# Router logits taken from the unnormalised stream, their transposes placed between output units, first gathers placed between the first expert units

## The chip, the core and the metric

The kernel runs on one core of one Trainium2 chip. The metric is device time in microseconds (us), lower is better. TensorE is called PE in the rows, VectorE DVE, ScalarE ACT, GpSimd POOL, and SP is the engine that issues most of the weight loads. TensorE's granted clock has two levels, 1.2 and 2.4 GHz; the rows give it as a share, 0.50 or 1.00.

## What is computed

One layer of a hybrid encoder over 16 meta tokens and 256 tokens, width 2048. The part that matters here is its second half: an output projection, a layer norm, a router, and a mixture of experts.

```python
h = layer_norm(ALPHA * h + mix, ln1_g[l], ln1_b[l])          # mix ends in: merged @ w_out
...
xf = h.reshape(n_tok, d)
g_logits = (xf @ w_group).astype(jnp.float32)                 # 4 groups
g_sel = jnp.argmax(g_logits + b_group.astype(jnp.float32), axis=-1)
...
e_logits = (xf @ w_expert).astype(jnp.float32).reshape(n_tok, N_GROUPS, EXPERTS_PER_GROUP)[tok, g_sel]
_, e_local = lax.top_k(e_logits + e_bias, TOP_K)              # 2 of the group's 8 experts
...
return (jax.nn.silu(xb @ w1[e]) * (xb @ w3[e])) @ w2[e]       # per expert, 32 experts, inner width 512
```

After the experts come a weighted sum of each token's two results, a residual and a last layer norm.

## The kernel before

**Units.** Every weight matrix is read in units of 1 MB (128 partitions x 2048 fp32). SP loads a unit, ACT copies it to its high part (`wh`, function `hi`), DVE subtracts to get the low part (`wl`, function `lo`), and PE multiplies with both parts. Before the experts PE uses 24 matmuls of 512 columns for a unit, in the expert part 8 (4 in full fp32 for two unsplit units in 24, `XR`). The expert part has 384 units, 24 per pair of experts, in 16 pairs (`pair`), and a ring of 8 units (`RING2`) whose high parts have 4 places (`HELD`).

**Order.** Each engine has a fixed program, written out by hand; engines wait for each other by semaphores. Nothing is rescheduled. An engine that waits holds up everything that stands behind in its own program.

**Output stage.** 16 units of `w_out` in four groups of four (`for j in range(4)` in the PE block). Each group gives 512 columns of the stream for both 128-token tiles, into two PSUM banks. DVE's `copy_out(j)` copies them to `mrg` and takes bn_stats. Group 3's copy can start only when the last unit is done.

**Between the last output unit and the first expert unit.** DVE normalises `mrg` in place (three passes over two tiles: mean and deviation, gain, bias) and splits the result into `xh1` and `xl1`. PE transposes `mrg` (32 transposes, `tensor_experts`, L822), ACT copies them out (L502), and PE multiplies with the router weights `wr` (32 matmuls of 36 columns, L828). DVE then selects group and experts in small dependent steps (`first_max`), PE counts ranks (L833 to L835), and DVE writes the 0/1 matrix `pg` for the first pair of experts (`gather_matrix`, L679).

**Gathers.** `gather(g, q)` on PE picks the tokens of pair g with `pg` out of `xh1` and `xl1`: 8 matmuls of 128 columns for each q, and q runs from 0 to 7. ACT copies each result to `xg` (`gathered`, L517). Before, PE does all 8 for pair 0 ahead of the first unit, while DVE computes the combine weights (small steps, L689 to L716). The gathers of pair 1 stand between the units of pair 0 (`G_FIRST`), and so on. An up-unit u reads only the gathers 2u and 2u+1. `pg` is one buffer: the matrix of the next pair is written when the last gather of this pair is done.

**Expert loop.** In pair 0 the units are called 0 to 19 here (k = 0 to 3, then 8 to 23). At the end of unit 8 (k = 12) PE runs `mix` (16 small matmuls, L891), which stands once at the same place in each pair and so marks the pairs in time.

Of the kernel before, what the change touches and what calls it, by code (L numbers as in the profile page):

```python
# [13 lines left out]
P = 128  # L14
# [77 lines left out]
def moe_trunk(nc, ins, out):  # L92
# [15 lines left out]
    with ctx:  # L108
# [176 lines left out]
        h1t = place("h1t", [P, KD, SEQ], 147456)  # L285
# [14 lines left out]
        pg = place("pg", [P, TT, 2 * SLOTS], M0 + 6144, F32R)  # L300
# [14 lines left out]
        ex = place("ex", [P, TT, 2], K0 + 5120)  # L315
        slots2 = place("slots2", [P, 2 * SLOTS], K0 + 2560)
# [14 lines left out]
        s_h1 = sem("s_h1")  # L331
        s_xh1 = sem("s_xh1")
        s_xl1 = sem("s_xl1")
        s_h1t = sem("s_h1t")
        s_h1tc = sem("s_h1tc")
# [62 lines left out]
        G_FIRST = (1, 3, 8, 10, 16, 18, 20, 22)  # L398

        def sync_experts(sp):  # L400
            def load(turn, x, src):

                n = 24 * turn + x if isinstance(turn, int) else None
                if n is not None and n < RING2:
                    if n < 4:
                        sp.wait_ge(s_ob, 2 * RET_PAIRS + 1)
                    else:
# [51 lines left out]
        def stage_constants(pool):  # L459

            pool.wait_ge(s_m, 9)
            for dst, src in ((ln1g[:, :], ins["ln1_g"].broadcast_to([P, D_MODEL])),
# [7 lines left out]
                pool.dma_start(dst, src).then_inc(s_c2, 16)  # L470
            nc.gpsimd.iota(tokm[:, :], [[P, TT]], -OUTSIDE, 1,
                           allow_small_or_imprecise_dtypes=True).then_inc(s_tok, 1)

        def pool_experts(pool):
            def scatter(filled, par):

                pool.wait_ge(s_h1, 1)
# [19 lines left out]
        def scalar_experts(act):  # L497

            act.wait_ge(s_wused, N_UNITS)
            for b in range(KD):  # L500
                act.wait_ge(s_h1t, b + 1)
                nc.scalar.activation(h1t[:, b, :], ps[:, b % 8, 0:SEQ], ACT.Copy).then_inc(s_h1tc, 1)  # L502
# [59 lines left out]
            def one_round(turn, ready=0):  # L562
                for x in range(ready, HELD):
                    hi(turn, x)
                pair(turn, 0, first=True)
# [8 lines left out]
            for x in range(HELD):  # L574
                hi(0, x)
            for n in range(2):
                act.wait_ge(s_r1, n + 1)
                dst = eg if n == 0 else ex
                nc.scalar.activation(dst[:, :, :], dst[:, :, :], ACT.Exp).then_inc(s_r2, 1)
            for q in range(8):  # L580
                gathered(0, 0, q)
            one_round(0, ready=HELD)
# [6 lines left out]
        def vector_experts(dve, own):  # L589

            for t in range(TT):
                if t == 0:
                    own.after(nc.vector.memset(gap[:, :], 0.0))
# [4 lines left out]
            for t in range(TT):  # L598
                s = nc.vector.tensor_scalar(mrg[:, t, :], mrg[:, t, :], mv[:, t, 0:1], rstd[:, t:t + 1],
                                            ALU.subtract, ALU.mult)  # L600
            own.after(s)
            dve.wait_ge(s_c2, 160)
            for t in range(TT):
                s = nc.vector.tensor_tensor(mrg[:, t, :], mrg[:, t, :], ln1g[:, :], ALU.mult)
            own.after(s)
            for t in range(TT):
                s = nc.vector.tensor_tensor(mrg[:, t, :], mrg[:, t, :], ln1b[:, :], ALU.add)
            s.then_inc(s_h1, 1)
            dve.wait_ge(s_h1, 1)
            dve.wait_ge(s_wused, N_UNITS)  # L610
            h1 = mrg[:, :, :].rearrange("q t (p k) -> q t k p", k=KD)
            for t in range(TT):
                nc.vector.tensor_scalar_mul(xh1[:, t, :, :], h1[:, t, :, :], 1.0).then_inc(s_xh1, 1)
            for t in range(TT):
                dve.wait_ge(s_xh1, t + 1)
                nc.vector.tensor_tensor(xl1[:, t, :, :], h1[:, t, :, :], xh1[:, t, :, :].bitcast(F32),
                                        ALU.subtract).then_inc(s_xl1, 1)
# [7 lines left out]

            for x in range(2):
                lo(0, x)
# [16 lines left out]
            own.after(nc.vector.tensor_copy(lg[:, :, :], ps[:, 6:8, 0:G + E]))  # L644
# [4 lines left out]
            own.after(nc.vector.tensor_reduce(rs[:, 2:4], gl, AXX, ALU.max))  # L649
            nc.vector.tensor_tensor(eg[:, :, :], gl, b3(rs[:, 2:4], G), ALU.subtract).then_inc(s_r1, 1)  # L650
            dve.wait_ge(s_r2, 1)
            own.after(nc.vector.tensor_reduce(rs[:, 4:6], eg[:, :, :], AXX, ALU.add))
            own.after(nc.vector.tensor_tensor(r2[:, :, 0:G], eg[:, :, :], ohg[:, :, :], ALU.mult))
            own.after(nc.vector.tensor_reduce(rs[:, 6:8], r2[:, :, 0:G], AXX, ALU.add))
            own.after(nc.vector.reciprocal(rs[:, 4:6], rs[:, 4:6]))
            own.after(nc.vector.tensor_tensor(rs[:, 6:8], rs[:, 6:8], rs[:, 4:6], ALU.mult))

            own.after(nc.vector.tensor_scalar(eg[:, :, :], ohg[:, :, :], -1.0, 1e30, ALU.add, ALU.mult))
            own.after(nc.vector.tensor_tensor(r1[:, :, :], el, brt[:, G:G + E].unsqueeze(1).broadcast_to([P, TT, E]), ALU.add))
            r14 = r1[:, :, :].rearrange("p t (g e) -> p t g e", g=G)  # L660
            own.after(nc.vector.tensor_tensor(r14, r14, eg[:, :, :].unsqueeze(3).broadcast_to([P, TT, G, PER_GROUP]), ALU.add))
# [5 lines left out]
            dve.wait_ge(s_asg, 1)  # L667
            own.after(nc.vector.tensor_scalar(r1[:, :, :], asg[:, :, :], -1000.0, 1000.0, ALU.mult, ALU.add))
# [17 lines left out]
            dve.wait_ge(s_mxr, 1)  # L686

            for k, oh in enumerate((oh1, oh2)):
                own.after(nc.vector.tensor_tensor(r2[:, :, :], oh[:, :, :], el, ALU.mult))  # L689
                own.after(nc.vector.tensor_reduce(rs[:, 10 + 2 * k:12 + 2 * k], r2[:, :, :], AXX, ALU.add))  # L690
            own.after(nc.vector.tensor_tensor(rs[:, 14:16], rs[:, 10:12], rs[:, 12:14], ALU.max))
            nc.vector.tensor_tensor(ex[:, :, 0], rs[:, 10:12], rs[:, 14:16], ALU.subtract)
            nc.vector.tensor_tensor(ex[:, :, 1], rs[:, 12:14], rs[:, 14:16], ALU.subtract).then_inc(s_r1, 1)

            dve.wait_ge(s_mxt, 1)
            own.after(nc.vector.tensor_reduce(nxf[:, 0:1], ps[0:1, 5, 0:P], AXX, ALU.max))
            own.after(nc.vector.tensor_scalar(nxf[:, 1:2], nxf[:, 0:1], float(SLOTS), None, ALU.is_gt))
            own.after(nc.vector.scalar_tensor_tensor(nxf[:, 2:3], nxf[:, 0:1], float(2 * SLOTS), nxf[:, 1:2], ALU.is_gt, ALU.add))
            own.after(nc.vector.scalar_tensor_tensor(nxf[:, 3:4], nxf[:, 0:1], float(3 * SLOTS), nxf[:, 2:3], ALU.is_gt, ALU.add))
            nc.vector.tensor_copy(nxi[:, 0:1], nxf[:, 3:4]).then_inc(s_nx, 1)  # L700
            for x in range(2, HELD):
                lo(0, x)

            dve.wait_ge(s_r2, 2)
            own.after(nc.vector.tensor_tensor(rs[:, 16:18], ex[:, :, 0], ex[:, :, 1], ALU.add))
            own.after(nc.vector.reciprocal(rs[:, 16:18], rs[:, 16:18]))
            own.after(nc.vector.tensor_tensor(rs[:, 16:18], rs[:, 16:18], rs[:, 6:8], ALU.mult))
            own.after(nc.vector.tensor_tensor(ex[:, :, :], ex[:, :, :], b3(rs[:, 16:18], 2), ALU.mult))
            own.after(nc.vector.tensor_tensor(wt[:, :, :], oh1[:, :, :], ex[:, :, 0:1].broadcast_to([P, TT, E]), ALU.mult))
            own.after(nc.vector.tensor_tensor(r2[:, :, :], oh2[:, :, :], ex[:, :, 1:2].broadcast_to([P, TT, E]), ALU.mult))  # L710
# [1245 lines left out]
```

## Time and profile before

| | us |
|---|---|
| median of 3 runs | 2248.09 |
| lowest, highest | 2244.63, 2248.26 |
| the profiled execution | 2248.71 |
| span of its records | 2246.6 |
| PE busy | 2124.5 (95%) |
| DVE busy | 1573.4 (70%) |
| ACT busy | 1238.8 (55%) |
| output stage, first to last matmul | about 1047.5 to 1147.1 |
| first expert unit starts | 1207.15 |

The span is read on one time axis, from its start. The views used below are: windows (busy time of each engine in a stretch, with the granted clock and the DMA), the timeline (groups of instructions in order of time; in brackets how long the engine sat idle before and for whom), and the list of DMA issues. A matmul's own duration overlaps the next one, so PE's pace is read from start to start, or from a whole group.

### The profile page before, as it was taken

The numbers are of one execution on the slowest core, as the hardware profiler recorded it, in microseconds if no ns is written. First come the engines' busy times: TensorE is split into PE (matmuls) and PEld (weight loads), VectorE is DVE, ScalarE is ACT, GpSimd is POOL, SyncE is SP. The second block draws the span as 40 slices with busy tenths as digits, with TensorE's granted clock in tenths as the row PEclk, the third lists the DMA queues.
The fourth block names the chain that finished last, engine by engine and source line by source line (L and its number), as shares of the span: only waits on it lengthen the run. The fifth ranks groups of instructions, "written<-read, shape, count | busy, mean of one in ns | idle before, by whom it ended". The sixth has DMA issues, their size and how long they took to land.

```text
span 2246.6 us, 30190 instructions
## 1 busy us (share of the span) xinstructions
PE 2124.5 (95%) x11513; PEld 1773.6 (79%) x11513; DVE 1573.4 (70%) x1348; ACT 1238.8 (55%) x1007; POOL 107.8 (5%) x76
## 2 busy tenths in 40 slices
PE   6999999999999999999978999999999999999991
PEld 5998777899998987887867777778777778777770
DVE  6545444453546365544466999989999999999986
ACT  3434443333232323333334888878887878888870
POOL 1000000000000000001000000000000000000001
PEclk9999999999999999999977999999999999999995
DMA  5554334655454544555544999999999999999973
GB/s 186 150 142 159 95 112 150 209 180 177 148 171 145 167 150 145 196 188 192 173 168 171 410 412 418 412 397 420 420 420 410 415 417 413 417 404 421 407 313 152
DMA packets 161974, 598.23 MB, mean 266 GB/s; under 512 B 20016, under 2 KB 28320, under 8 KB 110544
## 3 DMA queue, kind: packets, MB, share of 16 engines
q1 hardware_dynamic: 158224, 589.60, 69.2%
q0 software_dynamic: 3680, 7.64, 1.0%
q8 instruction: 50, 0.82, 0.1%
q14 instruction: 20, 0.16, 0.0%
HBM read 590.90 MB, written 18.87 MB: 271 GB/s over the span
## 4 chain that ended last, share of the span: by engine, by line
PE 74%; DVE 13%; issue 9%; ACT 2%; DMA 1%; POOL 1%; DVEq 0%; SPq 0%; POOLq 0%; ACTq 0%
PE ps L1551 20%; PE ps L1535 14%; PE ps L869 9%; DVE wl L623 9%; PE ps L870 9%; PE ps L866 5%; PE ps L850 3%; PE ps L891 3%; PE ps L1642 2%; PE ps L1622 2%; ACT wh L512 1%; PE ps L1609 1%; DVE yall L748 1%; PE ps L1663 1%; DMA yrow<-yscr 1%
## 5 line engine op out<-in xcount | busy, mean ns | idle before, releaser
L623 DVE TENSOR_TENSOR wl<-raw,wh 128x2048 fp32r<-128x2048 f32 x352 | 786.6, 2286 | 58.7 <-ACT wh L512 57.4
L512 ACT ACTIVATE wh<-raw 128x2048 fp32r<-128x2048 f32 x352 | 664.8, 1912 | 122.2 <-PE ps L870 71.9
L1198 DVE TENSOR_TENSOR wl<-raw,wh 128x2048 fp32r<-128x2048 f32 (+1 forms) x169 | 382.2, 2264 | 310.2 <-ACT wh L1031 310.2
L1031 ACT ACTIVATE wh<-raw 128x2048 fp32r<-128x2048 f32 (+1 forms) x169 | 319.9, 1896 | 463.4 <-DMA raw<-in_w_in_dram 283.6
L869 PE MATMUL ps<-wh,xg 128*128 128x512 f32 x900 | 382.4, 425 | 0.8 <-issue 0.7
L870 PE MATMUL ps<-wl,xg 128*128 128x512 f32 x900 | 359.4, 399 | 0.0
L1535 PE MATMUL ps<-hth,wh 128*128 128x272 f32 (+1 forms) x896 | 260.0, 290 | 5.0 <-DVE wl L1198 3.6
L1535 PE MATMUL ps<-htl,wh 128*128 128x272 f32 (+1 forms) x896 | 256.9, 287 | 0.0
L1535 PE MATMUL ps<-hth,wl 128*128 128x272 f32 (+1 forms) x896 | 256.8, 287 | 0.0
L869 PEld LDWEIGHTS ps<-wh,xg 128*128 128x128 f32 x900 | 173.4, 193 | 52.4 <-DVE wl L623 9.7
L869 PE MATMUL ps<-wh,hx 128*128 128x512 f32 x508 | 204.6, 403 | 3.4 <-DVE hx L741 3.4
L870 PEld LDWEIGHTS ps<-wl,xg 128*128 128x128 f32 x900 | 173.6, 193 | 40.6 <-issue 7.4
L870 PE MATMUL ps<-wl,hx 128*128 128x512 f32 x508 | 200.1, 394 | 0.0
L1535 PEld LDWEIGHTS ps<-hth,wh 128*128 128x128 f32 x896 | 169.5, 189 | 8.0 <-issue 3.5
L1535 PEld LDWEIGHTS ps<-htl,wh 128*128 128x128 f32 x896 | 169.4, 189 | 0.3
L1535 PEld LDWEIGHTS ps<-hth,wl 128*128 128x128 f32 x896 | 169.1, 189 | 0.0
L1551 PE MATMUL ps<-wh,hth 128*128 128x512 f32 x384 | 154.6, 403 | 0.0
L1551 PE MATMUL ps<-wh,htl 128*128 128x512 f32 x384 | 151.0, 393 | 0.0
L1551 PE MATMUL ps<-wl,hth 128*128 128x512 f32 x384 | 150.9, 393 | 0.0
L479 POOL DMA_INDIRECT yscr<-yall,dest x32 | 73.3, 2292 | 980.1 <-DVE yall L748 980.1
L869 PEld LDWEIGHTS ps<-wh,hx 128*128 128x128 f32 x508 | 96.4, 190 | 23.1 <-DVE hx L741 3.5
L866 PE MATMUL ps<-raw,xg 128*128 128x512 f32 x248 | 113.3, 600 | 0.0
(315 smaller groups left out, 3105.0 us busy)
## 6 DMA issues: line engine op xcount, KB each, us to landing
raw<-in_w_dram SPq DMA_DIRECT2D x384, 1024.0 KB, 8.1
raw<-in_w_in_dram SPq DMA_DIRECT2D x104, 1024.0 KB, 5.1
raw<-in_w_pa_dram SPq DMA_DIRECT2D x16, 1024.0 KB, 5.1
raw<-in_w_pb_dram SPq DMA_DIRECT2D x16, 1024.0 KB, 5.1
raw<-in_w_out_dram SPq DMA_DIRECT2D x16, 1024.0 KB, 5.1
raw<-in_w_ukv_dram SPq DMA_DIRECT2D x8, 1024.0 KB, 5.4
yrow<-yscr SPq DMA_DIRECT2D x4, 1024.0 KB, 9.8
raw<-in_w_uq_dram SPq DMA_DIRECT2D x8, 384.0 KB, 3.6
```

The lines of the kernel that those rows point to most:

```text
L479: pool.indirect_dma_start(yscr[:, :], bass.IndirectOffsetOnAxis(dest[0:SLOTS, par:par + 1], 0), yall[0:SLOTS, par, :], None, bounds_check= ...
L512: nc.scalar.activation(wh2[:, x % HELD, :], raw2[:, slot2(x), :], ACT.Copy).then_inc(s_wh2, 1)
L623: nc.vector.tensor_tensor(wl2[:, slot2(x), :], raw2[:, slot2(x), :], wh2[:, x % HELD, :].bitcast(F32), ALU.subtract).then_inc(s_wl2, 1)
L850: m = nc.tensor.matmul(bank[:, b, :, h, :], src[:, t, 2 * q + b, :], pg[:, t, :].rearrange("p (a s) -> p a s", a=2), start=t == 0, stop=t ...
L866: m = nc.tensor.matmul(o, s.bitcast(F32), raw2[:, slot2(x), c:c + 512], start=st, stop=sp_, skip_group_check=True)
L869: nc.tensor.matmul(o, s, wh2[:, x % HELD, c:c + 512], start=st, stop=False, skip_group_check=True)
L870: m = nc.tensor.matmul(o, s, wl2[:, slot2(x), c:c + 512], start=False, stop=sp_, skip_group_check=True)
L891: nc.tensor.matmul(ps[:, 6, c:c + SLOTS], ab[:, v, P * f:P * (f + 1)], fold[:, :], start=True, stop=True, skip_group_check=True)
L1031: nc.scalar.activation(wh[:, n % RING1, 0:c], raw1[:, n % RING1, 0:c], ACT.Copy).then_inc(s_wh, 1)
L1198: nc.vector.tensor_tensor(wl[:, n % RING1, 0:c], raw1[:, n % RING1, 0:c], wh[:, n % RING1, 0:c].bitcast(F32), ALU.subtract).then_inc(s_wl, 1)
L1535: m = nc.tensor.matmul(ps[:, bank, col:col + width], w[:, n % RING1, c:c + P], s[:, 4 * u + k, c0:c0 + width], start=opens and u == 0 and ...
L1551: m = nc.tensor.matmul(ps[:, bank + t, :], s[:, 4 * u + k, c:c + P], w[:, n % RING1, 512 * k:512 * (k + 1)], start=u == 0 and k == 0 and j ...
```

## The change

**Router logits.** The stream y (before the norm) is transposed instead of the normalised one, and multiplied with `gwr` = gain x `wr`. With mean and deviation per token, logits = rstd x (y @ gwr - mean x sum(gwr)) + sum(bias x wr). Both sums come from `router_sums` on DVE and one matmul with `ones` on PE. Transposes (`turn_stream(j)`), their copy on ACT (`turned(j)`) and the matmuls (`logits(j)`) of groups 0 to 2 stand between output units of the next group; those of group 3 follow the last unit.

**Norm.** It becomes two passes per tile: (y - mean) x gain ahead of the logits, and x rstd + bias (`stream(t)`), of which one tile stands after the expert choice, the other after `pg`. `xh1` moves from DVE to ACT.

**First gathers.** Gathers 2k and 2k+1 of pair 0 stand ahead of unit k, k = 0 to 3. `combine_weights` (DVE), with the two exponentials on ACT, moves behind the low part of unit 5. The first splits, and pair 1's `gather_matrix`, move too. `G_FIRST` has 8, 9, 10, 11 for 1, 3, 8, 10.

**Loads.** `yt` lies over two slots of the ring, so units 2 and 3 wait for the logits, and two loads of single elements (`g1t`, `b1t`) are added on POOL's queue.

```diff
-        G_FIRST = (1, 3, 8, 10, 16, 18, 20, 22)
+        G_FIRST = (8, 9, 10, 11, 16, 18, 20, 22)
...
+            turned(3)
+            hi(0, 0)
+            hi(0, 1)
+            for t in range(TT):
+                act.wait_ge(s_h1, t + 1)
+                nc.scalar.activation(xh1[:, t, :, :], mrg[:, t, :].rearrange("q (p k) -> q k p", k=KD),
+                                     ACT.Copy).then_inc(s_xh1, 1)
+            for u in range(4):
+                gathered(0, 0, 2 * u)
+                gathered(0, 0, 2 * u + 1)
+                if u < 2:
+                    hi(0, 2 + u)
+            one_round(0, early=weights_exp)
...
             def pair(turn, p, first=False, early=None):
                 for x in body(first):
                     k = step(x, first)
-                    if k == 0 and first:
+                    lo(turn, x + HELD)
+                    if k == 1 and early:
+                        early()
+                    if k == 3 and first:
                         gather_matrix(turn + 1, 2 * p + 2)
-                    lo(turn, x + HELD)
...
             def pair(turn, par, first=False, early=False):
+                    if early and k < 4:
+                        gather(0, 2 * k)
+                        gather(0, 2 * k + 1)
+                        pe.wait_ge(s_xg, 2 * k + 2)
...
             def turn_stream(j):
                 pe.wait_ge(s_co, 2 * j + 2)
                 for t in range(TT):
                     for b in range(4):
                         m = nc.tensor.transpose(ps[:, 2 * j + b // 2, SEQ * (b % 2) + P * t:SEQ * (b % 2) + P * (t + 1)],
                                                 mrg[:, t, 512 * j + P * b:512 * j + P * (b + 1)], ident[:, :])
                 m.then_inc(s_yt, 1)
...
+                    if j and u == 1:
+                        turn_stream(j - 1)
+                    if j and u == 2:
+                        logits(j - 1)
```

**DVE, from the last copy of the output stage on.** `wl` is a low part, `xl` is `xl1`, `r`, `rs`, `oh`, `asg` are the selection's small tiles. Before:

```order
L596 TENSOR_SCALAR var<-mv 128x2
L599 TENSOR_SCALAR mrg<-mrg,mv,rstd 128x2048 x2
L604 TENSOR_TENSOR mrg<-mrg,ln1g 128x2048 x2
L607 TENSOR_TENSOR mrg<-mrg,ln1b 128x2048 x2
L613 TENSOR_SCALAR xh_124<-mrg 128x2048 x2
L616 TENSOR_TENSOR xl_125<-mrg,xh_124 128x2048 x2
L623 TENSOR_TENSOR wl_122<-raw_121,wh_123 128x2048 x2
L644 COPY lg<-ps 128x72
```

The same place on DVE in the change:

```order
L621 TENSOR_SCALAR var<-mv 128x2
L622 TENSOR_SCALAR negmu<-mv 128x2
L625 SCALAR_TENSOR_TENSOR mrg<-mrg,negmu,ln1g 128x2048 x2
L664 SCALAR_TENSOR_TENSOR lraw<-wsumb,negmu,ps 128x36 x2
L668 SCALAR_TENSOR_TENSOR lg<-lraw,rstd,wsumb 128x36 x2
```

Five double passes and two low parts stood ahead of the selection (L644 on); one double pass stands there now, and the rest behind it.

**DVE in the first pair, behind the selection.** Before, from the last small steps on:

```order
L711 TENSOR_TENSOR wd<-wt,r_149 128x64
L713 SCALAR_TENSOR_TENSOR wd<-oh_152,tokm 128x64
L716 MEMSET beyond 128x1
L679 TENSOR_TENSOR pg<-slots_156,rk__144 128x256
L623 TENSOR_TENSOR wl_122<-raw_121,wh_123 128x2048 x6
```

In the change:

```order
L638 TENSOR_TENSOR xl_125<-mrg,xh_124 128x2048 x2
L645 TENSOR_TENSOR wl_122<-raw_121,wh_123 128x2048 x6
L712 TENSOR_REDUCE rs<-lg 128x2
...
L746 MEMSET beyond 128x1
L645 TENSOR_TENSOR wl_122<-raw_121,wh_123 128x2048 x2
L697 TENSOR_TENSOR pg<-slots_165,rk__152 128x256
```

`pg` for pair 1 stood ahead of the low parts of units 4 and up; it now stands behind those of units 0 to 7 and behind the 28 small steps L712 to L746.

**ACT, the same place.** Before:

```order
L512 ACTIVATE wh_123<-raw_121 128x2048 x4
L579 ACT_TABLE_LOAD
L579 ACTIVATE eg<-eg 128x8
L579 ACTIVATE ex<-ex 128x4
L517 ACTIVATE xg<-ps 128x512 x8
L512 ACTIVATE wh_123<-raw_121 128x2048 x2
```

In the change:

```order
L602 ACTIVATE xh_124<-mrg 128x2048 x2
L530 ACTIVATE xg<-ps 128x512 x2
L525 ACTIVATE wh_123<-raw_121 128x2048
L530 ACTIVATE xg<-ps 128x512 x2
L525 ACTIVATE wh_123<-raw_121 128x2048
L530 ACTIVATE xg<-ps 128x512 x4
L525 ACTIVATE wh_123<-raw_121 128x2048 x2
L595 ACT_TABLE_LOAD
L595 ACTIVATE eg<-eg 128x8
L595 ACTIVATE ex<-ex 128x4
L525 ACTIVATE wh_123<-raw_121 128x2048 x2
```

The high parts of units 4 and 5 stand behind all eight gather copies in both; what differs is that the last of these copies now waits for PE to have run units 0 to 2.

## Rows read from the trace of the kernel before

**Rows 1.** Windows: stretch, length, PE, PEld, DVE, ACT, POOL busy, clock, DMA share, GB/s.

```profile
1080.00:1100.00 20.00, 20.00 (x98) 16.85 (x97) 7.21 (x4) 6.39 (x4) 0.00 (x0) 1.00 0.49 160
...
1597.45:1658.90 61.45, 60.16 (x299) 47.54 (x297) 58.76 (x41) 51.79 (x40) 4.50 (x2) 1.00 1.01 420
...
1720.35:1781.80 61.45, 60.97 (x296) 48.47 (x295) 57.16 (x38) 50.18 (x39) 4.51 (x2) 0.97 1.01 412
```

**Rows 2.** Timeline, the pairs' marks: start, duration, instruction, in brackets idle before.

```profile
1659.51 1.99 PE L891 MATMUL ps<-fold,ab 128*128 128x64 f32 x16 [0.96 <-DVE wdc L724]
...
1720.12 1.99 PE L891 MATMUL ps<-fold,ab 128*128 128x64 f32 x16 [0.98 <-DVE wdc L724]
...
1782.28 1.99 PE L891 MATMUL ps<-fold,ab 128*128 128x64 f32 x16 [0.96 <-DVE wdc L724]
```

**Rows 3.** Timeline, DVE between the last output unit and the router.

```profile
1147.29 1.22 DVE L1491 COPY mrg<-ps 128x1024 f32<-128x1024 f32 x1 [14.94 <-PE ps L1880]
...
1151.61 2.60 DVE L599 TENSOR_SCALAR mrg<-mrg,mv,rstd 128x2048 f32<-128x2048 f32 x2 [1.14 <-POOL rstd L1511]
1154.25 4.49 DVE L604 TENSOR_TENSOR mrg<-mrg,ln1g 128x2048 f32<-128x2048 f32 x2
...
1167.00 7.29 DVE L616 TENSOR_TENSOR xl<-mrg,xh 128x2048 fp32r<-128x2048 f32 x2
```

**Rows 4.** Timeline, PE's transposes ahead of the output stage and the router's own.

```profile
1041.16 4.12 PE L1857 MATMUL ps<-ident,mrg 128*128 128x128 f32 x32 [2.68 <-DVE mrg L1362]
...
1163.32 6.54 PE L822 MATMUL ps<-ident,mrg 128*128 128x128 f32 x32 [16.07 <-DVE mrg L607]
...
1170.54 12.00 PE L828 MATMUL ps<-wr,h1t 128*128 128x36 f32 x64 [0.68 <-ACT h1t L502]
```

**Rows 5.** Timeline, DVE's selection, ranks and first small steps of the weights.

```profile
1182.85 0.17 DVE L647 TENSOR_TENSOR r<-lg,brt 128x8 f32<-128x8 f32 x1
...
1184.04 0.16 DVE L649 TENSOR_REDUCE rs<-lg 128x2 f32<-128x8 f32 x1
...
1185.66 0.17 DVE L658 TENSOR_SCALAR eg<-ohg 128x8 f32<-128x8 f32 x1
...
1189.22 0.23 DVE L666 TENSOR_TENSOR asg<-oh,oh 128x64 f32<-128x64 f32 x1
...
1191.10 0.23 DVE L671 TENSOR_TENSOR rk__144<-ps,r 128x64 f32<-128x64 f32 x1 [1.43 <-PE ps L835]
...
1192.41 0.22 DVE L689 TENSOR_TENSOR r<-oh,lg 128x64 f32<-128x64 f32 x1
...
1194.69 4.47 DVE L623 TENSOR_TENSOR wl<-raw,wh 128x2048 fp32r<-128x2048 f32 x2
```

**Rows 6.** Timeline, PE: first gather, units 0 and 1, a gather, pair 0's mark.

```profile
1192.53 0.66 PE L850 MATMUL ps<-pg,xh 128*128 128x128 f32 x2
...
1207.15 0.77 PE L869 MATMUL ps<-wh,xg 128*128 128x512 f32 x1 [0.73 <-issue]
...
1210.43 0.40 PE L869 MATMUL ps<-wh,xg 128*128 128x512 f32 x1
...
1212.27 0.33 PE L850 MATMUL ps<-pg,xh 128*128 128x128 f32 x2
...
1228.75 1.89 PE L891 MATMUL ps<-fold,ab 128*128 128x64 f32 x16
```

**Rows 7.** Timeline, ACT and DVE: high part, low parts of units 4 to 8.

```profile
1210.69 3.75 ACT L512 ACTIVATE wh<-raw 128x2048 fp32r<-128x2048 f32 x2 [3.64 <-PE ps L870]
...
1212.64 11.48 DVE L623 TENSOR_TENSOR wl<-raw,wh 128x2048 fp32r<-128x2048 f32 x5 [5.70 <-ACT wh L512]
```

**Rows 8.** Windows as in rows 1, where the granted clock changes.

```profile
1152.00:1154.00 2.00, 0.00 (x0) 0.00 (x0) 2.00 (x2) 0.00 (x0) 0.00 (x0) 0.52 0.97 410
...
1168.00:1170.00 2.00, 1.86 (x12) 1.62 (x10) 2.00 (x1) 1.88 (x6) 0.00 (x0) 0.71 0.00 0
...
1210.00:1212.00 2.00, 2.00 (x10) 1.67 (x9) 0.00 (x0) 1.31 (x1) 0.00 (x0) 0.97 0.35 49
```

**Rows 9.** DMA issues: tiles, queue, size, median us from issue to landing.

```profile
wr<-in_w_group_dram POOLq DMA_DIRECT2D x1, 32.0 KB, 9.2
```

More of the change, by code:

```diff
@@ L495, in pool_experts, with scalar_experts @@
             nc.gpsimd.tensor_tensor(marks[:, 5:6], half[:, 0:1], half[:, 0:1], ALU.mult).then_inc(s_all, 1)
[L497 to L502, printed above, removed]
+        def scalar_experts(act, turned):
             def hi(turn, x):
@@ L560, in pair, with one_round @@
                             gathered(turn + 1, 1 - par, q)
[L562 to L565, printed above, removed]
+            def one_round(turn, early=None):
+                if not early:
+                    for x in range(HELD):
+                        hi(turn, x)
+                pair(turn, 0, first=True, early=early)
                 pair(turn + 1, 1)
@@ L572, in one_round, with weights_exp @@
                 outputs(last, 23, 2 * last + 1, 1, last)
[L574 to L582, printed above, removed]
+            def weights_exp():
+                for n in range(2):
+                    act.wait_ge(s_r1, n + 1)
+                    dst = eg if n == 0 else ex
+                    nc.scalar.activation(dst[:, :, :], dst[:, :, :], ACT.Exp).then_inc(s_r2, 1)
+            turned(3)
[11 more added lines that the diff above has]
+            one_round(0, early=weights_exp)
             act.wait_ge(s_nx, 1)
@@ L643, in vector_experts @@
             dve.wait_ge(s_lg, 1)
-            own.after(nc.vector.tensor_copy(lg[:, :, :], ps[:, 6:8, 0:G + E]))
+            for t in range(TT):
+                s = nc.vector.scalar_tensor_tensor(lraw[:, t, :], wsumb[:, 0, :], negmu[:, t:t + 1],
+                                                   ps[:, t, 0:G + E], ALU.mult, ALU.add)
+            own.after(s)
+            for t in range(TT):
+                s = nc.vector.scalar_tensor_tensor(lg[:, t, :], lraw[:, t, :], rstd[:, t:t + 1], wsumb[:, 1, :],
+                                                   ALU.mult, ALU.add)
+            own.after(s)
             gl, el = lg[:, :, 0:G], lg[:, :, G:G + E]
@@ L692, in vector_experts @@
[L692 to L698, printed above, removed]
@@ L768, in pair, with one_round @@
                         output_rest(2 * turn, 0)
-            def one_round(turn, ready=0):
-                for x in range(ready, HELD):
-                    lo(turn, x)
-                pair(turn, 0, first=True)
+            def one_round(turn, early=None):
+                if not early:
+                    for x in range(HELD):
+                        lo(turn, x)
+                pair(turn, 0, first=True, early=early)
                 with dve.Fori(1, PAIRS) as p:
@@ L778, in one_round @@
                 output_rest(2 * last + 1, 1)
-            one_round(0, ready=HELD)
+            one_round(0, early=combine_weights)
             dve.wait_ge(s_nx, 1)
@@ L896, in mix, with pair @@
                 m.then_inc(s_hm, 1)
-            def pair(turn, par, first=False):
+            def pair(turn, par, first=False, early=False):
                 for x in body(first):
@@ L949, in one_round @@
                 pe.wait_ge(s_ye[1], last + 1)
-            for q in range(8):
-                gather(0, q)
-            pe.wait_ge(s_nx, 1)
-            one_round(0)
+            pe.wait_ge(s_xl1, TT)
+            one_round(0, early=True)
             more = pe.value_load(nxi[0:1, 0:1], min_val=0, max_val=ROUNDS - 1)
```

240 lines of the change are left out of this document (149 added, 91 removed).

## The prediction

> **What bounds the kernel now.** I read the windows first [rows 1]. In the output stage PE is busy for all of 20 us at full clock while ACT and DVE idle for two thirds of the time, so PE work added there moves the end of the stage one for one. In the expert stage PE, DVE and the DMA are all near full, so the marks of the pairs have to say which one rules [rows 2]. From mark to mark an undisturbed pair takes 60.6 us (1659.51 to 1720.12); the next takes 62.2 (1720.12 to 1782.28), and the window that nearly covers it has the clock at 0.97 instead of 1.00. The 1.6 us are not made up, and the DMA falls from 420 to 412 GB/s. A ring of eight units would swallow 1.6 us of slower PE if the DMA ruled. So I take the expert stage as a fixed length behind pair 0's mark at 1228.75 [rows 6], whatever moves that mark moves the end, and the whole sum is made at that mark.
>
> Between the last unit of the output stage (DVE takes over at 1147.29 [rows 3]) and the first expert unit (1207.15 [rows 6]) PE mostly waits for a chain through DVE: norm, split, router, selection, ranks. The loads of the first 8 units are in long before.
>
> **1. Output stage: longer.** Per group the change adds 8 transposes and 8 matmuls of 36 columns on PE, for three groups ahead of the last unit. 32 transposes took at most 4.12 at full clock, where ACT held them up towards the end, and 6.54 mostly at half clock; the 32 router matmuls took 12.0, most of it at half clock [rows 4]. A quarter at full clock is then about 0.9 for the transposes and, with half of 12.0/4 and a little for the part that already ran fast, 1.7 for the matmuls. Three times 2.6 is 7.8; the matmul with `ones` makes it 8.1. PE has no pause to hide it. Bounds: 6 (small matmuls at full clock cheaper than half) and 9. Group 3's copy starts at 1147.3 + 8.1 = 1155.4.
>
> The rest added there costs nothing: `router_sums` and `turned` stand on DVE and ACT, 64% and 68% idle [rows 1]. The two single-element loads are of the kind of `w_group`, which landed in 9.2 us [rows 9]; they are issued with it, before the output stage, and DVE first asks for them behind the low part of its fifth unit.
>
> **2. Chain to the first gather: shorter.** From the copy to the end of `var` DVE was busy 1151.61 - 1147.29 - 1.14 = 3.2 [rows 3]; with two half copies and `negmu` 3.6, so 1159.0. A 2048-column pass on DVE is 4.49/2 = 2.25 [rows 3]; I take 2.3 for the new fused passes. Two of them: 1163.6. Group 3's transposes and logits (0.9, an ACT copy of about 1.0, 1.7 to 3.3) run beside this. Four small steps 0.9: 1164.5. The selection was 1182.85 to 1189.45, of which 1184.04 to 1185.66 moves behind [rows 5]: 6.6 - 1.6 = 5.0, so 1169.5. `stream(0)` 2.3, which covers PE's ranks: 1171.8. Ranks to `pg` and maximum, 1191.10 to 1192.41 [rows 5] and a step: 1.5, 1173.3. `stream(1)` 2.3: 1175.6. `xl1` 7.3 [rows 3]: 1182.9. ACT's `xh1` runs beside it; no row shows it. From below it costs a plain copy, 1.9 [rows 7]; from above that times the 3.65/2.25 that DVE pays for the same reordered read [rows 3], 3.1. At either end it is ready before its reader. The first gather starts at 1183.0 instead of 1192.5.
>
> **3. First units: earlier, in a slower rhythm.** Two gathers at half clock: 13.6/4 = 3.4 (from 1192.53 to 0.7 ahead of 1207.15), then 0.7 for ACT's copy, which now stands ahead of each of four units. Unit 0 starts at 1187.1 instead of 1207.15, **20 us earlier**. It takes 3.4 at half clock (before 3.3, its tail already fast), so it ends at 1190.5. The clock in before fell about 5 us behind the last output matmul, stayed low through all 64 gather matmuls, and rose at 1210 in unit 0 [rows 6, 8]. I let it rise about 1191 here too. From then a round is 1.7 + 0.7 + 1.85 (unit 1 before: 1210.43 to 1212.27) = 4.25. Units 1 and 2 end at about 1195 and 1199.3, the last two gathers at 1201.0, their copy at 1201.7, unit 3 at 1203.5.
>
> **4. The new wait.** ACT's high part of unit 4 stands behind that last gather copy. DVE has had nothing since the low part of unit 3. From 1201.7: high part 1.9 [rows 7], low parts of 4 and 5 4.5, then `combine_weights`: 12 of its steps took 1192.41 to 1194.69, the 7 moved ones 1.6 [rows 5], so 28 are 5.7; low parts of 6 and 7 4.5; `pg` of pair 1 0.45. That is 17.1, so `pg` is there at 1218.8. PE has unit 4 done by about 1208, and next in its program is pair 1's first gather, which waits for `pg`. Queued behind it are units 5 to 8, though 5's low part is ready since 1208. PE **idles about 10.5 us**, where before it never stopped. The reason it did not: `pg` was written ahead of unit 4's low part, and the 28 steps ran while PE gathered. DVE is no later than before (low parts to 8 at 1224.1 [rows 7], now 1221 or so); PE is behind.
>
> **5. To pair 0's mark.** From 1218.8: four gathers 3.4, units 5 to 8 7.5; the clock has fallen again, and getting it back costs half of some 5 us, 2.6; `mix` waits about 0.5 for the last gather copy. 14.0, so 1232.8 against 1228.75: **+4.1 us**. In one line: +8.1 in the output stage, -17.6 on the chain to the first gather, and +13.6 between first gather and mark.
>
> The profiled execution took 2248.71, 2.1 above its span and 0.6 above the median of 2248.09. 2248.1 + 4.1 gives 2252.2; I say **2252.5**.
>
> A rule of the Trainium skill bears on step 1 and on the clock. The rows show the clock rising at 1169.3 after nothing but transposes had run since 1163.32 [rows 4, 8]. "TensorE: Matmul & The Clock Gate", Part 4, says that transposes do not count as busy for the gate and do not bring full clock. By that rule the trace should have stayed low there; it did not, so I give the rule little. Its own result is the fourth rival.
>
> **The rivals.**
> *The DMA rules the expert stage: no slower.* For it: share 1.01 and the same 420 GB/s in undisturbed pairs [rows 1]. Against it: the 1.6 us not made up [rows 2]. Its price: the ring refills from unit 0's end. Before that is 1210.4, with 2.5 us for a unit of 1.05 MB, so by 1232.8 the DMA had moved 9.0 units. Now it fetches the five behind units 0 to 4, stops, and goes on from unit 5's end at about 1224: by 1232.8 it has 5 + 3.5 = 8.5. It trails by 0.5 units: +1.2 us, 2249.3. Decisive is whether a pair stays at 60.6 behind a late mark.
> *PE stays slow through units 1 to 3: slower still.* Each round is then 7.5 instead of 4.25; two rounds and the last gathers make 8 more, 2260. For it: 64 gathers did not raise the clock. Against it: 2.8 us of unit 0 did.
> *The wait for `pg` does not bind: faster.* If PE ran on from 1203.5 it would need 5 units and 4 gathers, 12.8, and reach the mark at 1216.3, 12.4 early: 2235.7. That needs DVE to write `pg` before 1206, though six low parts and 28 steps stand ahead of it. Only if the change does not order DVE as it reads.
> *Transposes let the clock fall in the output stage.* Each of three falls would cost 1.6 (what one costs a pair [rows 2]): +4.9 on top, 2257.
>
> **How the numbers follow.** The forecast with its own range (2249.5 to 2256) 0.52, DMA 0.15, slow rounds 0.18, faster 0.08, transposes 0.07. Own range: -2.1 for cheap small matmuls, +1 for dear ones, 1 either way for where the clock rises. The clock's drops in the expert stage cost 1.6 each and their number may change by one or two: this blurs every case by 2. About 0.2%, 4.5 us, is what a measurement of this kernel can tell from no change, and the forecast lies just below that: half of it and of the blur falls on either side. Slower: 0.25 + 0.18 + 0.06 = 0.49. Faster: 0.08 and some luck from the blur, 0.11. The same: 0.40. Range: 2247 (cheap matmuls and the DMA case) to 2261 (slow rounds), which leaves out the fast case and a tail.
>
> **What would show it.** Last output unit ending at 1155 (step 1; 1153 or 1157 would re-size it). First gather near 1183 and unit 0 near 1187 (2). Rounds of 4.3 or of 7.5 from unit 1 on (3). An idle PE of about 10 us with DVE's `pg` as releaser, ahead of pair 1's first gather (4). Pair 0's mark near 1233, pairs of 60.6 or 62.2 behind it (5). I am wrong if PE runs through from unit 4 to the mark, if the output stage ends below 1152, or if pairs shorten behind a late mark.

## The result, and the profile after

The changed kernel takes **2256.69 us** (median of 11 runs, 2251.25 to 2261.82), the kernel before 2248.33 (11 runs, 2244.63 to 2249.85). The ratio is 1.0035, interval 1.0026 to 1.0043: **slower by 0.35%**, where I forecast 2252.5, slower at 0.49 and the same at 0.40, and a range of 2247 to 2261. The median lies in that range, and 0.7 above the narrower one (2249.5 to 2256) that I gave the forecast itself. The profiled execution took 2255.36, its span 2253.6.

The table compares the two profiled executions at the points of the sum.

| point | before | forecast | after |
|---|---|---|---|
| copy of group 3 starts | 1147.29 | 1155.4 | 1156.29 |
| first gather | 1192.53 | 1183.0 | 1183.55 |
| unit 0 | 1207.15 | 1187.1 | 1187.91 |
| `pg` of pair 1 is written | not in PE's way | 1218.8 | 1220.14 |
| pair 0's mark | 1228.75 | 1232.8 | 1234.73 |
| pair 15's mark | 2150.58 | | 2156.63 |
| end of the span | 2246.6 | | 2253.6 |

First the added router work of one group, in PE's timeline (start, duration, instruction, in brackets the idle time before it and what ended it):

```profile
1082.35 0.34 PE L1964 MATMUL ps<-wsum,ones 128*128 128x72 f32 x2
...
1088.07 1.03 PE L1925 MATMUL ps<-ident,mrg 128*128 128x128 f32 x8
...
1094.40 1.87 PE L1934 MATMUL ps<-gwr,yt 128*128 128x36 f32 x16
```

8 transposes and 8 router matmuls (the trace has two records for each of these) take 2.90 us a group. The window over them has PE busy for all of 20 us at full clock, as [rows 1] had it (length; PE, PEld, DVE, ACT, POOL busy; clock; DMA share; GB/s):

```profile
1080.00:1100.00 20.00, 20.00 (x103) 16.93 (x102) 7.93 (x6) 6.35 (x4) 0.00 (x0) 1.00 0.46 158
```

So 3 x 2.90 + 0.34 is 9.0, and DVE's copy of group 3 starts 9.0 later than in [rows 3]. DVE's chain behind it:

```profile
1156.29 1.29 DVE L1528 COPY mrg<-ps 128x512 f32<-128x512 f32 x2 [17.46 <-PE ps L1958]
...
1159.50 4.61 DVE L625 SCALAR_TENSOR_TENSOR mrg<-mrg,negmu,ln1g 128x2048 f32<-128x2048 f32 x2
1164.15 0.41 DVE L664 SCALAR_TENSOR_TENSOR lraw<-wsumb,negmu,ps 128x36 f32<-128x36 f32 x2
...
1169.81 0.23 DVE L683 TENSOR_TENSOR asg<-oh,oh 128x64 f32<-128x64 f32 x1
...
1176.23 7.27 DVE L638 TENSOR_TENSOR xl<-mrg,xh 128x2048 fp32r<-128x2048 f32 x2
```

There is no idle bracket from the copy to the last row: DVE waits for nobody. Before, it waited 1.14 for POOL [rows 3], 1.43 for PE's ranks [rows 5] and, most of all, for the router that PE runs behind its 32 transposes:

```profile
1182.58 0.23 DVE L644 COPY lg<-ps 128x72 f32<-128x72 f32 x1 [3.89 <-PE ps L828]
```

From copy to first gather the chain is 18.0 us shorter. Some 6.7 of it are these waits and a short one for ACT; two low parts that now stand behind are another 4.5; the rest is DVE work that is dropped, given to ACT or moved behind. That is the half of the change that works. The other half is in PE's timeline, in rows that begin behind an idle time:

```profile
1183.55 0.69 PE L869 MATMUL ps<-pg,xh 128*128 128x128 f32 x2 [11.98 <-DVE xl L638]
...
1187.91 0.79 PE L888 MATMUL ps<-wh,xg 128*128 128x512 f32 x1 [0.69 <-ACT xg L530]
...
1194.57 0.50 PE L888 MATMUL ps<-wh,xg 128*128 128x512 f32 x1 [0.69 <-ACT xg L530]
...
1199.11 0.50 PE L888 MATMUL ps<-wh,xg 128*128 128x512 f32 x1 [0.69 <-ACT xg L530]
...
1207.78 0.50 PE L888 MATMUL ps<-wh,xg 128*128 128x512 f32 x1 [1.90 <-DVE wl L645]
...
1220.19 0.69 PE L869 MATMUL ps<-pg,xh 128*128 128x128 f32 x2 [10.30 <-DVE pg L697]
...
1234.73 1.97 PE L910 MATMUL ps<-fold,ab 128*128 128x64 f32 x16 [0.33 <-ACT xg L530]
```

Unit 0 starts 19.2 us earlier than in [rows 6], and the mark comes 6.0 later. The row at 1220.19 holds the reason: PE stood for 10.3 us until DVE had written `pg` of pair 1. DVE in that time:

```profile
1205.43 4.49 DVE L645 TENSOR_TENSOR wl<-raw,wh 128x2048 fp32r<-128x2048 f32 x2 [6.79 <-ACT wh L525]
1209.84 0.16 DVE L712 TENSOR_REDUCE rs<-lg 128x2 f32<-128x8 f32 x1
...
1215.21 0.06 DVE L746 MEMSET beyond<- 128x1 f32 x1
1215.31 4.49 DVE L645 TENSOR_TENSOR wl<-raw,wh 128x2048 fp32r<-128x2048 f32 x2
1219.72 0.42 DVE L697 TENSOR_TENSOR pg<-slots,rk__152 128x256 fp32r<-128x256 f32 x1
```

It first idled 6.79 us for ACT's high part of unit 4, then did two low parts, the small steps of the weights (1209.84 to 1215.27) and two more low parts. The two engines wait for each other in turn.

Behind the mark nothing is won back. PE runs `mix` twice in a pair, once for each expert; the marks here and in [rows 2] are the first of the two. Three marks of the expert stage, the second of the two pairs between them undisturbed:

```profile
1357.80 1.44 PE L910 MATMUL ps<-fold,ab 128*128 128x64 f32 x11 [0.96 <-DVE wdc L754]
...
1419.99 1.99 PE L910 MATMUL ps<-fold,ab 128*128 128x64 f32 x16 [0.96 <-DVE wdc L754]
1480.61 1.99 PE L910 MATMUL ps<-fold,ab 128*128 128x64 f32 x16 [0.99 <-DVE wdc L754]
```

An undisturbed pair is 60.62 here (1419.99 to 1480.61) as in [rows 2], others are 62.2 (1357.80 to 1419.99), and from pair 0's to pair 15's mark it is 921.90 against 921.83 before.

### The profile page after: what moved, and what is told of

Its sections match the earlier page's. It is cut to its first block, busy times and chain, and to the rows that moved or that the text cites. A ratio compares the mean times of both kernels' runs of the same rounds, so it can differ in the third digit from the quotient of the medians.

```text
span 2253.6 us, 30198 instructions
## 1 busy us (share of the span) xinstructions
PE 2117.6 (94%) x11515; PEld 1767.5 (78%) x11515; DVE 1572.2 (70%) x1356; ACT 1244.7 (55%) x997; POOL 110.0 (5%) x78
## 4 chain that ended last, share of the span: by engine, by line
PE 73%; DVE 17%; issue 6%; ACT 3%; DMA 1%; POOL 0%; DVEq 0%; SPq 0%; POOLq 0%; ACTq 0%
PE ps L1607 20%; PE ps L1591 14%; DVE wl L645 12%; PE ps L888 7%; PE ps L889 7%; PE ps L885 5%; PE ps L1958 4%; PE ps L910 3%; PE ps L869 2%; ACT wh L525 2%; PE ps L1698 2%; PE ps L1678 1%; DVE yall L778 1%; PE ps L1665 1%; PE ps L1719 1%
## 5 line engine op out<-in xcount | busy, mean ns | idle before, releaser
L869 PE MATMUL ps<-pg,xh 128*128 128x128 f32 x544 | 100.1, 266 | 22.3 <-DVE xl L638 12.0
L869 PEld LDWEIGHTS ps<-pg,xh 128*128 128x128 f32 x544 | 94.3, 195 | 33.2 <-DVE xl L638 12.1
```

Source lines behind the costliest of these rows:

```text
L869: m = nc.tensor.matmul(bank[:, b, :, h, :], src[:, t, 2 * q + b, :], pg[:, t, :].rearrange("p (a s) -> p a s", a=2), start=t == 0, stop=t ...
```

## The experiments

All seven start from the changed kernel. Theory: its first half (router logits from the raw stream) gains on the chain to the first gather more than it costs in the output stage; its second half (gathers between the first units) loses more than that, because `pg` of pair 1 and the steps of the weights now stand on DVE where PE has nothing else to do. Rivals: the DMA sets the length of the expert stage; PE's clock sets it. The kernel before was run again beside them and is at 2249.51 (first four) and 2249.15 (last three) instead of 2248.33; the changed kernel was not, so each distance to it below may be 0.8 to 1.2 larger than given.

**Only `pg` of pair 1 earlier**, behind the low part of unit 3.

```
+            gather_matrix(1, 2)
...
-                    if k == 3 and first:
+                    if k == 3 and first and not early:
                         gather_matrix(turn + 1, 2 * p + 2)
```

> The changed kernel with one move: DVE writes pg of pair 1 right behind the low part of unit 3 instead of behind that of unit 7; the 28 small steps stay where they are. Theory (the wait for pg stops PE ahead of pair 1's first gather): the idle 10.3 us goes there, but units 6 and up then wait about 4.5 us for their low parts, which still stand behind the 28 steps. Pair 0's mark at about 1225.5 instead of 1234.7, total 8 to 10 below the changed kernel, about 2248, level with the kernel before. Rival (DVE as a whole is late and PE only shows it): the low parts of units 8 and up come no earlier, the gain is at most the 5.4 us that DVE idles behind unit 8's low part, total 2251 to 2254.

2249.56 (2246.2 to 2255.24), beside 2249.51 for the kernel before: ratio 1.0002 (0.9992 to 1.0012), 7.1 below the changed kernel. PE's timeline:

```profile
1197.80 0.79 PE L889 MATMUL ps<-wh,xg 128*128 128x512 f32 x1 [0.69 <-ACT xg L530]
...
1204.62 0.50 PE L889 MATMUL ps<-wh,xg 128*128 128x512 f32 x1 [0.69 <-ACT xg L530]
...
1223.16 0.77 PE L889 MATMUL ps<-wh,xg 128*128 128x512 f32 x1 [4.21 <-DVE wl L645]
...
1232.65 1.97 PE L911 MATMUL ps<-fold,ab 128*128 128x64 f32 x16 [0.33 <-ACT xg L530]
```

The window behind the pause (length; PE, PEld, DVE, ACT, POOL busy; clock; DMA share; GB/s):

```profile
1223.00:1227.00 4.00, 3.84 (x12) 3.09 (x12) 4.00 (x3) 2.96 (x4) 0.00 (x0) 0.57 0.01 2
```

The 10.3 us in front of the gather are gone and 4.2 us in front of unit 6 have come: its low part stands behind the 28 steps. So moving `pg` uncovers the second wait, as the theory had it. The mark missed its number in this execution by 7.1 (1232.65 for 1225.5). Everything up to the first gather was 2.1 later. The clock rose later: from unit 0 to 1 it took 7.77 instead of 6.66, and from unit 1 to 2 6.82 instead of 4.54, 3.4 in all. The remaining 1.6 fits the window above: the clock was at half again behind the pause ahead of unit 6. The median, over 10 runs, came within 1.6 of its number, and below the 2251 to 2254 of the rival. This trace alone, with its mark only 2.1 earlier, would not refute that rival; the third experiment does.

**Only the weights earlier.** The steps are split; the first part goes behind the low part of unit 1, the rest behind that of unit 2; PE's transpose of the maxima goes behind the ranks, and ACT's exponentials behind the first two gather copies and the high part of unit 2.

```
+            lo(0, 0)
+            lo(0, 1)
+            scores()
+            lo(0, 2)
+            combine_weights()
+            lo(0, 3)
...
-                    if k == 1 and early:
-                        early()
```

> The changed kernel with the other half: the 28 small steps, with the two exponentials on ACT and the small transpose on PE, stand between the low parts of units 1 and 3, where DVE idles in the changed kernel; pg of pair 1 stays behind the low part of unit 7. Theory: pg comes 5 us earlier (1214.9), PE idles 5.3 instead of 10.3 us, mark at 1229 to 1230, total 5 below the changed kernel (up to 7 if the shorter pause keeps the clock up), about 2251. Rival (the steps' place costs nothing, only pg's order does): no change against the changed kernel.

2250.66 (2248.8 to 2254.23), ratio 1.0008 (0.9998 to 1.0017), 6.0 below the changed kernel. PE's timeline:

```profile
1217.84 0.69 PE L875 MATMUL ps<-pg,xh 128*128 128x128 f32 x2 [4.83 <-DVE pg L697]
...
1232.38 1.97 PE L916 MATMUL ps<-fold,ab 128*128 128x64 f32 x16 [0.34 <-ACT xg L530]
```

The wait for `pg` shrinks by 5.5, about the length of the 28 steps (5.4), and the time by 6.0. What is left, 4.8, is about two low parts. The mark missed its number here too, 1232.38 for 1229 to 1230: the clock rose later as in the first experiment (7.77 from unit 0 to 1, 6.85 from unit 1 to 2), 3.4 in all. In this execution 3.3 fell away again behind the mark (918.64 from there to pair 15's, instead of 921.90), two falls of the clock fewer, which made up for it.

**Both earlier.** The two edits together.

> Both moves of the two kernels before together: 28 small steps between the low parts of units 1 and 3, pg of pair 1 behind that of unit 3. Theory: PE does not stop from unit 4 to the mark except 1.9 us ahead of unit 4; the mark at about 1221, 13.7 below the changed kernel's, total about 2243, 5 below the kernel before. If the DMA ruled the expert stage, the end could not follow the mark by all of this: 2 to 3 us would be given back in the pairs behind it (pairs of 61 to 62 us instead of 60.6).

2243.06 (2241.58 to 2244.32), ratio 0.9969 (0.9959 to 0.9979): faster than before. PE's timeline from the first gather:

```profile
1186.88 0.69 PE L876 MATMUL ps<-pg,xh 128*128 128x128 f32 x2 [9.29 <-DVE xl L638]
...
1210.57 0.50 PE L895 MATMUL ps<-wh,xg 128*128 128x512 f32 x1 [2.03 <-DVE wl L645]
...
1225.53 1.97 PE L917 MATMUL ps<-fold,ab 128*128 128x64 f32 x16 [0.33 <-ACT xg L530]
```

Between unit 4 at 1210.57 and the mark PE no longer stands for DVE. From first gather to mark it is 38.65, against 51.18 in the changed kernel: 12.5 less, and the medians say 13.6. The total given ahead, 2243, was met; the mark given ahead, 1221, was not. It came at 1225.53, of which 3.3 stood there at the first gather already: the clock was at 0.50 from 1048 to 1058, ahead of everything that this experiment touches. Part of that came back behind the mark (920.16 instead of 921.90), so some luck is in the total. The 9 runs lie within 2.7 us.

**The first half of the change alone.** All 8 gathers ahead of unit 0 as before, `pg` of pair 1 and the steps of the weights on DVE while PE gathers.

```
-        G_FIRST = (8, 9, 10, 11, 16, 18, 20, 22)
+        G_FIRST = (1, 3, 8, 10, 16, 18, 20, 22)
...
+            for q in range(8):
+                gather(0, q)
             one_round(0, early=True)
```

> The change's first half alone: router logits from the raw stream and the new norm as in the changed kernel, but all eight gathers of pair 0 ahead of unit 0 and those of pair 1 where they were before, with the 28 small steps beside the gathers. Theory: first gather at 1183.5 as in the changed kernel, from there 36.2 us to pair 0's mark as in the kernel before: mark about 1219.8, total about 2242, 14 to 15 below the changed kernel and 6 below the kernel before. This would put the whole loss on the second half of the change. Rival (the output stage's longer PE work is what makes it slow): the total stays above the kernel before's.

2239.46 (2239.23 to 2240.2), ratio 0.9956 (0.9939 to 0.9972). PE's timeline:

```profile
1183.66 0.69 PE L874 MATMUL ps<-pg,xh 128*128 128x128 f32 x2 [9.35 <-DVE xl L636]
...
1198.26 0.79 PE L893 MATMUL ps<-wh,xg 128*128 128x512 f32 x1 [0.69 <-ACT xg L530]
...
1221.26 1.89 PE L915 MATMUL ps<-fold,ab 128*128 128x64 f32 x16
```

Unit 0 starts 10.3 later than in the changed kernel and the mark comes 13.5 earlier. From first gather to mark it is 37.60. So the first half alone gains 10.0 us in medians (2249.51 to 2239.46; 7.5 of it stand at the profiled mark), and the second half costs 17.2 (2256.69 against 2239.46). Of these the order on DVE is 13.6, as the experiment before showed. The other 3.6 (2243.06 against 2239.46) remain with the gathers between the units even when DVE's order is right; the two traces show 1.1 of them between first gather and mark (38.65 against 37.60), and where the rest lies is not shown. My number was 2242, 2.5 too high.

**The router work of groups 0 to 2 behind the last output unit.** The other cost, tested by itself.

```
-                    if j and u == 1:
-                        turn_stream(j - 1)
-                    if j and u == 2:
-                        logits(j - 1)
...
-            turn_stream(3)
-            logits(3)
+            for j in range(4):
+                turn_stream(j)
+            for j in range(4):
+                logits(j)
```

> Compared with the changed kernel, the transposes and router matmuls of groups 0 to 2 (and the matmul with ones stays) move behind the last output unit, to where group 3's stand; nothing is left out. Theory (they cost PE 2.9 us per group in the output stage, where PE has no pause, and hide behind DVE's norm only in part): group 3's copy falls back from 1156.3 to 1147.5 to 1148; behind it PE has 32 transposes (4.1 at full clock) and 32 router matmuls (7.5 at full clock, up to 12 where the clock has fallen), so the logits are there at 1160 to 1164 while DVE asks for them at 1155.4: DVE waits 4.5 to 8.5 there. First gather at 1179.5 to 1183.5 instead of 1183.55, mark of pair 0 by as much earlier: time 2253 (2251 to 2257), 0 to 4 below the changed kernel's 2256.7. Rival (the router work hides wholly behind DVE's norm chain, so its place is the whole cost): first gather at 1175, time 2248. Rival (the 9 us in the output stage is not the router work but something else of the change, as the loads or the two new DVE passes): the copy stays at 1156 and the time rises to 2260 or more.

2251.98 (2248.49 to 2254.87, 10 runs) beside 2249.15 before, ratio 1.0016 (1.0006 to 1.0025), 4.7 below the changed kernel. PE's and then DVE's timeline:

```profile
1149.23 3.66 PE L1926 MATMUL ps<-ident,mrg 128*128 128x128 f32 x32
1152.73 8.95 PE L1935 MATMUL ps<-gwr,yt 128*128 128x36 f32 x64
```

```profile
1149.43 1.29 DVE L1529 COPY mrg<-ps 128x512 f32<-128x512 f32 x2 [14.58 <-PE ps L1959]
...
1161.82 0.41 DVE L665 SCALAR_TENSOR_TENSOR lraw<-wsumb,negmu,ps 128x36 f32<-128x36 f32 x2 [4.20 <-PE ps L1935]
```

The same work that costs 8.7 between the output units costs DVE a wait of 4.2 behind them (and 0.4 for the transposes), because DVE's norm covers the rest. The gain of 4.7 is a little more than the 0 to 4 expected, and the mark is 3.4 earlier (1231.31). The copy is at 1149.43 instead of the expected 1147.5 to 1148; in the next kernel it is at 1147.66. The two differ by one more fall of the clock, in the window ahead (length, PE busy, clock, DMA share, GB/s; this kernel, then the next):

```profile
1000.00:1047.00 47.00, 44.31 (x204) 0.96 0.61 203
```

```profile
1000.00:1047.00 47.00, 42.68 (x201) 1.00 0.62 210
```

**Both gains in one kernel.** The gathers first, and the router work late.

> The version with all 8 gathers ahead of unit 0 (2239.5) with the router work of groups 0 to 2 moved behind the last output unit as well; nothing is left out. Theory (the two edits act on one chain one after the other, so they add): the gain of the late router work over that version is the same 0 to 4 us: 2236.5 (2235 to 2240). First gather 1179.5 to 1183.5 instead of 1183.66, unit 0 14.6 later. Rival (moved work lets the clock fall or delays ranks, nothing is gained or some lost): 2239.5 to 2243.

**2236.9** (2235.58 to 2238.87, 4 runs) beside 2249.15, ratio 0.995 (0.9933 to 0.9967): 0.5% faster than the kernel before, 2.6 below the version with the gathers first alone. It is the best version. Its DVE and PE:

```profile
1147.66 1.29 DVE L1529 COPY mrg<-ps 128x512 f32<-128x512 f32 x2 [14.79 <-PE ps L1959]
...
1160.44 0.41 DVE L663 SCALAR_TENSOR_TENSOR lraw<-wsumb,negmu,ps 128x36 f32<-128x36 f32 x2 [4.60 <-PE ps L1935]
```

```profile
1217.29 1.89 PE L918 MATMUL ps<-fold,ab 128*128 128x64 f32 x16
```

DVE waits for the logits as in the version before, 4.60, and the mark is 4.0 earlier than with the gathers first alone. The late router work is worth 4.7 on the changed kernel and 2.6 here, the first somewhat above the 0 to 4 that were expected, the second inside; these runs cannot tell whether the two differ.

**The copy's order of reading.** ACT's copy of the stream took 3.70 us, outside my bounds. This kernel leaves out the order that the gather wants, so that it reads in a row.

```
-  ... mrg[:, t, :].rearrange("q (p k) -> q k p", k=KD),
+  ... mrg[:, t, :].rearrange("q (k p) -> q k p", k=KD),
```

> ACT's copy of the stream into its high part reads its 2048 columns in a row instead of in the transposed order (4-byte elements 64 bytes apart); the output is then no longer the reference's, since the high part stands in another order than the gather wants; nothing else changes, and the work of every engine stays the same in count. Theory (the order of the read alone makes ACT's copy take 3.70 us instead of 1.9): both copies fall to 1.9 each, so the first is there before DVE's first low part and the second 3.5 us before the second; DVE's two passes of 3.64 stay, and with them the first gather at about 1183.5 (1183.0 to 1183.6): 2256 +-3, no change in time. Rival (ACT is slow there for another reason, such as DVE's work on the same tile at the same time): the copies stay at 3.5 to 3.7. Rival (the low part waits for ACT's copy): first gather moves ahead by more than 1.

ACT's rows in the changed kernel, then in this one:

```profile
1172.45 7.40 ACT L602 ACTIVATE xh<-mrg 128x2048 fp32r<-128x2048 f32 x2 [9.07 <-DVE mrg L632]
```

```profile
1172.48 1.91 ACT L602 ACTIVATE xh<-mrg 128x2048 fp32r<-128x2048 f32 x1 [9.07 <-DVE mrg L632]
1176.16 1.91 ACT L602 ACTIVATE xh<-mrg 128x2048 fp32r<-128x2048 f32 x1 [1.76 <-DVE mrg L632]
```

The order of the read alone costs ACT 1.8 us on 2048 columns. The first gather moves by 0.3 (1183.23) and the mark by 0.1 (1234.65), so it was just hidden. The one run took 2251.69, 3.7 below the changed kernel's profiled execution and 5.0 below its median. 3.1 of the 3.7 lie behind the mark: from there to pair 15's it is 918.78 instead of 921.90, with two falls of the clock fewer.

## Why the forecast came out as it did

**Step 1, output stage: right in kind, 0.9 too small.** +9.0 for +8.1, at my upper bound. I took half of 12.0/4 for the matmuls and had 1.7; they took 1.87. The transposes took 1.03 for 0.9. The late version shows the 9.0 to be this work and nothing else: without it the copy of the last version is at 1147.66, 0.4 behind the 1147.29 of [rows 3], which is the 0.34 of the matmul with `ones`.

**Step 2, chain to the first gather: right.** From copy to first gather it is 27.26 for my 27.6 and 45.24 before. One bound was wrong and cost 0.3 at the first gather: ACT's reordered copy took 3.70, above the 3.1 I gave as the top. I had scaled ACT by DVE's ratio, 3.65/2.25 = 1.6; ACT's is 3.70/1.91 = 1.9. I had written that it is ready before its reader at either end; at 3.70 it is ready at the very moment, since two of them (7.40) end at 1179.85, when DVE has finished its first low part.

**Step 3, first units: right in kind, 1.4 too short.** Unit 0 is at 1187.91 for 1187.1. I let the clock rise at about 1191, within unit 0. It rose at about 1192.5, in the gathers behind unit 0:

```profile
1190.00:1192.00 2.00, 2.00 (x7) 1.61 (x7) 1.99 (x1) 0.00 (x0) 0.00 (x0) 0.50 0.00 0
1192.00:1194.00 2.00, 1.88 (x15) 1.74 (x14) 0.00 (x0) 0.68 (x2) 0.00 (x0) 0.87 0.65 139
```

So it took 6.66 from unit 0 to unit 1, where my sum has 5.8 (3.4 + 1.7 + 0.7). A round at full clock is 4.54 (1194.57 to 1199.11) for 4.25: two gathers take 1.9 for my 1.7, and the unit 1.96 for 1.85. The last gather copy was done at 1203.6 for 1201.7.

**Step 4, the new wait: right, in place, releaser and size.** 10.30 us for 10.5, released by DVE's `pg`. The 28 steps took 5.4 for 5.7. That DVE itself would be no later than before held too: its low parts are done up to unit 8 at 1222.3, against 1224.1 before. It is PE that is behind.

**Step 5, to the mark.** 14.5 from PE's restart to the mark for 14.0. The clock had fallen in the pause, as assumed. I had it at half for some 5 us without a row that says so; it was some 6:

```profile
1213.00:1220.00 7.00, 0.00 (x0) 0.00 (x0) 6.59 (x14) 4.68 (x4) 0.00 (x0) 0.50 0.14 61
1220.00:1226.00 6.00, 5.81 (x19) 5.04 (x20) 2.34 (x2) 0.82 (x2) 0.00 (x0) 0.50 0.00 0
```

In my one line, +8.1 - 17.6 + 13.6 = +4.1 has become +9.0 - 18.0 + 15.0 = **+6.0** at the mark. The terms that were too small are the output stage (0.9) and the stretch from first gather to mark (1.4: 1.4 more up to the last gather copy, where the clock rose late and gathers and rounds were longer, 0.6 less from there to `pg`, and 0.6 more behind it).

**Behind the mark.** +0.07 in 15 pairs, then +0.95 in the tail (96.97 for 96.02), and the time beyond the span is 0.35 less: 6.65 between the two profiled executions, 8.4 between the medians. The tail is the same code in all versions and took 95.8 to 97.5 in them, so the 0.95 is scatter and no part of the change; I did not find what makes it. The remaining 1.7 is that the profiled execution was 1.3 quicker than its kernel's median, and before's 0.4 slower than its own: the 11 runs spread over 10.6 us, where before's spread over 5.2. Their mean granted clock goes with it, 0.973 in the quickest and 0.968 in the slowest. That the new pauses of PE at the start make the clock rise at different moments fits the executions of the first two experiments, where it rose about a unit later, which cost 3.4. It also fits the third, in which PE no longer stands for `pg` and whose 9 runs spread over 2.7. For the changed kernel's own longer runs it is argued, not shown. I had also taken 4.5 us as the least that a measurement of this kernel can tell from no change. The interval is about 1.9 us to either side, so my odds gave "the same" more than it should have had.

**The rivals.** *The DMA rules the expert stage*: refuted. It would hand back part of a late mark in shorter pairs, and undisturbed pairs are 60.6 behind marks at 1217.29, 1225.53 and 1234.73 alike. Two marks behind the one at 1225.53, in the third experiment:

```profile
1286.27 1.97 PE L917 MATMUL ps<-fold,ab 128*128 128x64 f32 x16 [0.91 <-DVE wdc L761]
1346.89 1.99 PE L917 MATMUL ps<-fold,ab 128*128 128x64 f32 x16 [0.95 <-DVE wdc L761]
```

*Slow rounds*: not in the profiled execution; in the traces of the first two experiments one round was slow, not all, which costs 3.4 and not 8. Two of the changed kernel's 11 runs took 2259.65 and 2261.82; no trace says what made them long. *The wait for `pg` does not bind*: refuted by the row at 1220.19. I had also priced it too low: with the waits taken away the kernel is at 2243.06 and not at 2235.7, since from first gather to mark it takes 38.65 where I had 33.3 (1183.0 to 1216.3). *Transposes let the clock fall*: refuted. From 1058 to 1156 the clock is 1.00 in the traces of the changed kernel and of all five versions that keep this work between the output units. And in the late version 32 transposes in a row and the small matmuls behind them ran at full clock:

```profile
1149.30:1152.70 3.40, 3.40 (x33) 3.40 (x32) 3.10 (x8) 2.39 (x3) 0.07 (x1) 1.00 0.00 0
1152.80:1157.00 4.20, 4.20 (x40) 4.20 (x40) 4.00 (x2) 4.20 (x4) 0.85 (x1) 1.00 0.00 0
1157.00:1161.60 4.60, 4.60 (x27) 4.54 (x26) 0.61 (x1) 0.68 (x1) 0.00 (x0) 0.60 0.00 0
```

The clock did fall in the third window, at about 1158, behind the transposes and while PE was busy with matmuls of 36 columns. In the last version (at about 1155.8) and in the kernel before (at about 1172.6) it fell in the middle of these matmuls too. So something in this mix does let it fall in the end; which of the two kinds it was is open. The Trainium skill, "TensorE: Matmul & The Clock Gate", Part 4 ("PE-mode transpose"), says that transposes do not count as busy for the gate; by that rule the transposes would have let the clock fall. Against it stands the rise at about 1169.2 in [rows 8], behind transposes only; no run here separates the two.

## What to carry to other kernels

PE started its first unit 19 us earlier and won nothing by it, because the small steps that once ran on DVE under PE's preparation now stood between PE and its second batch. Before you move work forward, list what ran beside it, and move that forward too. A step of half a microsecond (`pg`) that stands behind four more low parts and 28 small steps made PE wait 10.3 us; moving it alone gave back 7.1, and moving both 13.6. And work put into a stage that has no pause costs its full length (8.7 us here), while behind that stage, beside another engine's chain, about half of it was free.

## What the runs showed of the hardware

- A copy on ACT of 2048 columns whose input elements lie 64 bytes apart took 3.70 us, in a row 1.91; DVE's subtraction with the same reordered read took 3.64, where the one for a unit's low part takes 2.29. The copy that moved to ACT had taken DVE 1.89 in the kernel before (3.78 for two), so the move doubled its own length; here that cost 0.3 at the first gather, since DVE was busy meanwhile.
- The clock's falls come as steps: a pair is 60.6 or 62.2, and in some traces, the first experiment's among them, one is 63.8, and the same work can have two falls more or fewer between two marks (921.90 and 918.78), which is as much as a 0.14% change of the kernel. Experiments on a few us have to be read at a mark ahead of the expert stage, or over many runs.
- In the pause of 10 us on PE (1209.9 to 1220.2) the clock was at 1.00 until about 1213 and at 0.50 from there on, and it stayed at 0.50 for some 6 us after PE had started again.
